# Expert weight slots read in longer contiguous rows: down slots of two experts by 256 features, gate and up slots of neighbouring channels

## The reference, cut to what matters

```python
def expert_choice_moe(xn, w_router, w_gate, w_up, w_down):
    cap = EC_CAPACITY_FACTOR * T // N_EXPERTS                 # 32
    aff = jax.nn.softmax((xn @ w_router), axis=-1)
    g, idx = lax.top_k(jnp.swapaxes(aff, 1, 2), cap)
    xs = xn[bidx, idx]                                        # (1, 16, 32, 1024)
    hid = jax.nn.silu(jnp.einsum('becd,edf->becf', xs, w_gate)) * jnp.einsum('becd,edf->becf', xs, w_up)
    y = jnp.einsum('becf,efd->becd', hid, w_down) * g[..., None]
    return jnp.zeros_like(xn).at[bidx, idx].add(y)
```

## Time and profile before

| | |
|---|---|
| median of 3 runs | 2414.48 us (2411.99 to 2416.81) |
| the profiled execution | 2415.41 us, span of its instructions 2413.6 us |
| mean granted TensorE clock | 0.948 |
| bytes read from HBM | 660.86 MB, of which the experts 402.7 MB |
| the mixture, first matmul L1391 to last L1414 | 409.6 to 1518 us |

### The profile page before, as it was taken

One profiled execution on the slowest core, in us unless ns is written; L12 is line 12 of the kernel. 1 busy time (PEld: TensorE's weight loads), 2 busy tenths in 40 slices (PEclk: granted clock), 3 DMA queues, 4 the chain that ended last, 5 costly groups with the idle time before them and its releaser, 6 DMA issues. The chain is left out here.

```text
span 2413.6 us, 32989 instructions
## 1 busy us (share of the span) xinstructions
PE 2087.0 (86%) x14348; PEld 1443.7 (60%) x14348; DVE 541.1 (22%) x1174; ACT 403.5 (17%) x737; POOL 185.0 (8%) x182
## 2 busy tenths in 40 slices
PE   6998888887687888888788787897999999899997
PEld 2674455554244545665356443674888877478886
DVE  4433432010332200000000210256300023632001
ACT  1122002021121200000000220235300023331001
POOL 0025000000100000000000000026000002330000
PEclk9999898999889999998999999999999999899999
DMA  9459757999999999999999999630254742124450
GB/s 371 162 212 377 283 197 309 412 400 413 409 401 410 415 403 408 412 409 412 405 414 416 415 390 409 202 132 1 95 185 120 164 161 97 60 71 140 130 158 26
DMA packets 239559, 664.03 MB, mean 275 GB/s; under 512 B 18359, under 2 KB 129368, under 8 KB 197112
## 3 DMA queue, kind: packets, MB, share of 16 engines
q1 hardware_dynamic: 239416, 661.93, 71.9%
HBM read 660.86 MB, written 1.05 MB: 274 GB/s over the span
## 5 line engine op out<-in xcount | busy, mean ns | idle before, releaser
L1045 PE MATMUL ps<-arena,ring 128*128 128x256 f32 x2240 | 484.8, 380 | 3.2 <-DVEq L370 3.2
L1045 PEld LDWEIGHTS ps<-arena,ring 128*128 128x128 f32 x2240 | 425.8, 190 | 62.0 <-DVEq L370 4.8
L608 PE MATMUL ps<-arena,ring 128*128 128x256 f32 (+2 forms) x1552 | 353.2, 389 | 15.1 <-DMA ring<-in_w_ffn_in 8.3
L1391 PE MATMUL ps<-ring,arena 128*32 128x256 f32 x4032 | 264.4, 410 | 85.9 <-DMA ring<-in_w_up 53.0
L608 PEld LDWEIGHTS ps<-arena,ring 128*128 128x128 f32 (+2 forms) x1552 | 278.1, 185 | 98.2 <-DMA ring<-in_w_ffn_in 22.1
L1391 PEld LDWEIGHTS ps<-ring,arena 128*32 128x32 f32 x4032 | 126.9, 116 | 209.6 <-DMA ring<-in_w_up 69.0
L1414 PE MATMUL ps<-ring,arena 128*32 128x512 f32 x1024 | 143.2, 684 | 88.1 <-DMA ring<-in_w_down 82.4
L1962 ACT ACTIVATE arena<-ps 128x512 f32<-128x512 f32 (+3 forms) x137 | 74.7, 545 | 774.7 <-PE ps L608 409.9
L1414 PEld LDWEIGHTS ps<-ring,arena 128*32 128x32 f32 x1024 | 29.6, 117 | 177.7 <-DMA ring<-in_w_down 118.5
L1118 PE MATMUL ps<-arena,ring 128*128 128x256 f32 x512 | 113.6, 384 | 5.0 <-issue 5.0
L1118 PEld LDWEIGHTS ps<-arena,ring 128*128 128x128 f32 x512 | 98.3, 193 | 22.2 <-issue 9.0
(11 more groups left out here) (338 smaller groups left out, 1771.3 us busy)
## 6 DMA issues: line engine op xcount, KB each, us to landing
ring<-in_w_up SPq DMA_DIRECT2D x64, 2048.0 KB, 14.0
ring<-in_w_down SPq DMA_DIRECT2D x64, 2048.0 KB, 15.1
ring<-in_w_gate SPq DMA_DIRECT2D x62, 2048.0 KB, 13.3
ring<-in_w_ada SPq DMA_DIRECT2D x36, 2048.0 KB, 12.1
ring<-in_w_ffn_in SPq DMA_DIRECT2D x64, 1024.0 KB, 7.9
ring<-in_w_ffn_out SPq DMA_DIRECT2D x16, 1408.0 KB, 7.0
ring<-in_w_in SPq DMA_DIRECT2D x9, 2048.0 KB, 9.1
ring<-in_w_out SPq DMA_DIRECT2D x6, 2048.0 KB, 7.8
```

The lines of the kernel that those rows point to most:

```text
L608: m = mm(o, a, x, start=(k == 0 and r == 0), stop=(k == kt - 1 and last))
L1045: m = mm(b, w[:, k, c:c + P], src[:, k, :], start=(k == 0), stop=(k == kt - 1))
L1391: m = mm(b[u][32 * c:32 * c + 32, T * x:T * x + T], xs[:, 2 * h + k, CAP * e:CAP * e + CAP], w[:, k, at_:at_ + T], start=(h == 0 and k == ...
```

## The change

Three sizes of row change, and with them the order of channels and features inside the slots. The number of slots, their bytes, their order in the stream and their places stay.

- Gate and up: slot h still holds channels 256h to 256h+255, but partition p now has channels 256h+2p and 256h+2p+1, which are neighbours in HBM: 16 KB in one piece for a partition, and the whole slot is 2 MiB in one piece.
- To match, the stationary operand of the `xs` matmuls takes every second channel of a block of 256 (stride of two floats).
- Down: a slot holds two experts and 256 features; partition p has features 256i+2p and 256i+2p+1 of each, 8 KB in one piece for each expert. Slots alternate between expert pairs a = 0 and 1.
- The transposes of `turn_hidden` take every second column of `hidm`.
- The down matmuls are as many and as large as before; bank a now holds the two experts of pair a, the column half n on partitions 64n to 64n+63. DVE empties each bank with two copies of 64 partitions x 512 columns in place of one of 128 x 512, so that `ysb` looks as before.
- Bank 0 of a group is closed by the last but one slot, bank 1 by the last.

```diff
--- before.py
+++ after.py
@@ -497,12 +497,13 @@
         for s, (kind, i) in enumerate(STEPS):
             if kind == "down":
                 g = i // 8
-                w = I["w_down"][0, 4 * g:4 * g + 4].rearrange("e (f p) n -> p f e n", p=P)
-                stream += [(f"down{g}_{f}", w[:, f]) for f in (2 * (i % 8), 2 * (i % 8) + 1)]
+                for a in range(2):
+                    w = I["w_down"][0, 4 * g + 2 * a:4 * g + 2 * a + 2].rearrange("e (f p s) n -> p f e (s n)", p=P, s=2)
+                    stream.append((f"down{g}_{2 * (i % 8) + a}", w[:, i % 8]))
             else:
                 e = i // 2
-                w = I["w_" + kind][0, e].rearrange("(k p) n -> p k n", p=P)
-                stream += [(f"{kind}{e}_{h}", w[:, 2 * h:2 * h + 2, :]) for h in (2 * (i % 2), 2 * (i % 2) + 1)]
+                w = I["w_" + kind][0, e].rearrange("(h p s) n -> p h s n", p=P, s=2)
+                stream += [(f"{kind}{e}_{h}", w[:, h]) for h in (2 * (i % 2), 2 * (i % 2) + 1)]
             if s in CTX_AT:
                 stream += CTX_STAGES[CTX_AT[s]][1]
         n_moe = len(stream)
@@ -1364,7 +1365,8 @@
             for k in range(KD):
                 b = open_bank(pe, f"xs{k}", MIX_BANKS)
                 for t in range(TT):
-                    m = mm(b[:], htok[:, t, P * k:P * k + P], sel[:, t].rearrange("p e s -> p (e s)"), start=(t == 0), stop=(t == 1))
+                    by_parity = htok[:, t].rearrange("p (h f s) -> p h s f", h=4, s=2)
+                    m = mm(b[:], by_parity[:, k // 2, k % 2], sel[:, t].rearrange("p e s -> p (e s)"), start=(t == 0), stop=(t == 1))
                 close_bank(m, f"xs{k}")
             for g2 in range(2):
                 if g2 == 0:
@@ -1402,22 +1404,25 @@
                 b = open_bank(pe, f"hd{e}", TURN_BANKS)
                 for u in range(2):
                     for x in range(2):
-                        m = nc.tensor.transpose(b[:, P * (2 * u + x):P * (2 * u + x) + P], hidm[u][:, P * x:P * x + P], ident)
+                        m = nc.tensor.transpose(b[:, P * (2 * u + x):P * (2 * u + x) + P], hidm[u].rearrange("p (f s) -> p s f", s=2)[:, x], ident)
                 close_bank(m, f"hd{e}")
 
             def down(g, f, b):
+                i, a = f // 2, f % 2
                 w = take(f"down{g}_{f}")
                 pe.wait_ge(hdt_ready, 4 * g + 4)
-                ch = 8 * (f // 8) + 4 * (f % 2) + f % 8 // 2
-                for n in range(2):
-                    for j in range(4):
-                        m = mm(b[n][32 * j:32 * j + 32, :], hdT[:, j, ch, :], w[:, j, W * n:W * n + W], start=(f == 0), stop=(f == 15))
-                    if f == 15:
-                        close_bank(m, f"dn{g}{n}")
-                if f < 15:
+                for odd in range(2):
+                    ch = 8 * (i // 4) + 4 * odd + i % 4
+                    for n in range(2):
+                        for j in range(2):
+                            at_ = D * odd + W * n
+                            m = mm(b[a][64 * n + 32 * j:64 * n + 32 * j + 32, :], hdT[:, 2 * a + j, ch, :], w[:, j, at_:at_ + W],
+                                   start=(i == 0 and odd == 0), stop=(i == 7 and odd == 1))
+                if i < 7:
                     release(m)
                 else:
-                    release_with(f"dn{g}1")
+                    close_bank(m, f"dn{g}{a}")
+                    release_with(f"dn{g}{a}")
 
             def combine(g, r, banks):
                 pe.wait_ge(ct_ready, 2)
@@ -1936,7 +1941,8 @@
                 elif kind == "down" and i % 8 == 7:
                     for n in range(2):
                         b = read_bank(dve, f"dn{g}{n}")
-                        step(v.tensor_copy(ysb[:, W * n:W * n + W], b[:]), frees=f"dn{g}{n}")
+                        step(v.tensor_copy(ysb[64 * n:64 * n + 64, 0:W], b[0:64, :]))
+                        step(v.tensor_copy(ysb[64 * n:64 * n + 64, W:2 * W], b[64:128, :]), frees=f"dn{g}{n}")
                         tell(y_evac)
                 ctx_stage(s)
             step(ts(A2[X], mod2[:, 0, 8:16, X], 1.0, None, ALU.add))
```

## The result

The changed kernel took 2398.18 us (median of 4, 2396.77 to 2400.21) beside 2415.24 us for the kernel before: ratio 0.9947, 95% interval 0.9925 to 0.9969 (the two medians alone would give 0.9929). That is 13 us less (7 to 18); 15.0 had been forecast. In a second set, with more runs of each, it was 0.9935 (0.9915 to 0.9955). The median of the first four runs lies 17 us lower, but the kernel before spreads over 2402 to 2419 us in what follows, so the ratios are the better measure.

The account below looks back on a forecast made before the run. The mixture was taken to be bound by how fast the 16 DMA engines move bytes. Of 18.6 us saved 15.8 arrive, less 0.8 for the evacuation: -15.0 us, 2399.5 us, range 2391 to 2411.

Parts of the forecast that it names:

- The bound: In the mixture of experts, time goes by how fast the 16 DMA engines move bytes; 409 GB/s from 420 to 1500 us.
- rival (2): PE takes the gain: faster loads wait more often for one of four ring places; 2413 to 2416 us; chance 0.10.
- The price of a row: Each row of a load costs a DMA engine 9.1 ns, beside 151.5 ns for 4 KB of bytes.
- Adjacent dimensions are merged: A partition's two neighbouring rows are sent as one piece though the view names them separately; 239559 packets less 32768.
- The down term: Down slots: 32768 rows of 4 KB become 16384 of 8 KB, saving each engine 9.3 us; bounds 8.6 to 12.4.
- the factor 0.87: Share of the loads' saving that arrives in the mixture: 13% is lost, so 18.2 us become 15.8.
- seven windows: Windows of 20 us with DMA share 0.97 to 0.99 in six, 0.89 in one; savings inside these 140 us are lost.
- The gate and up term: Gate and up slots: half as many rows, 16 KB for 8 KB, saving each engine 9.3 us; bounds 0 to 11.9.
- The evacuation: End of the last group: bank 1 takes two DVE copies of 0.69 us each, +0.8 us; bounds 0 to 0.8.
- The strided loads: Strided stationary operands of L1367 and the transposes: 0 us taken; upper bounds 6 us and under 1 us.
- (1): Half of the gain: 16 KB pieces bring nothing, or half of the 9.1 ns isn't the row's; 2407.2 us; chance 0.19.
- (3): Gate and up loads: 16 KB from partition to partition is bad spacing for memory; +11.5 us, 2426.0 us; chance 0.09.

Follow-up runs that it names:

- the part alone: Only the down change, or only the gate and up change, made to the kernel before: ratio 0.9964 (8.7 us less) and 0.9971 (7.0 us less).
- the ACT experiment: Changed kernel with ACT copying one half of the very last bank while DVE copies the other: ratio 0.9948 to the kernel before.
- the run of one expert: Changed kernel, but a down slot is one expert by 512 features in four 4 KB rows: ratio 0.9998 to the kernel before.

## Why the prediction was right

**The bound.** Right. In the down phases, and in the third and fourth of gate and up, time followed the bytes' rate in both directions (4, 8 and 16 KB). The waits of the earlier trace rows are those of PE and of its weight load together, as the first part of the prediction says; rival (2) is argued there with all 402 us, of which half is nearer to lost time.

**The price of a row.** Right. From 408, 421 and 427 GB/s an engine takes 160.6, 311.3 and 613.9 ns for a row of 4, 8 and 16 KB, so a row costs 9.9 ns by the first two and 8.8 by the last two, where 9.1 was taken. Neither the number of experts in a slot nor a contiguous slot had a part in it. Whether the price is that of the piece itself or of the jump to another address, no run separates.

**Adjacent dimensions are merged.** Right, 32768 packets fewer.

**The down term.** 8.1 us were to arrive (9.3 x 0.87). The down phases of the two traces of after are 8.3 us shorter than the mean of the three of before, and the part alone gained 8.7 (5.5 to 12) in time. That the factor 0.87 fits is luck: of the seven windows behind it none lies in a down phase.

**The gate and up term.** 7.7 us were to arrive (8.9 x 0.87). In time the part alone gained 7.0 (3.6 to 10.4), which agrees. In the traces it is 731.4 to 726.4, 5.0 us, and 7.2 in the trace of the part alone. The sum was about right; the way to it was not. The prediction lost only what falls inside seven windows of 20 us, 13% of the stretch, and kept "what they saved before". Six of the seven (from 420, 480, 500, 680, 700 and 740 us) lie in the first and second phase, 120 of their 353 us, so two thirds of the 4.6 us saved there were to be kept; by the traces above it is 0.9 us. The third and fourth passed on all of their 2.3 us each (2.7 and 2.4), though the seventh window lies in the fourth. The whole mixture became 11 to 13 us shorter, where 15.8 was to arrive. The rows: phases 1 to 4 of gate and up, first in the second trace of before, then after.

```profile
403.50:580.50 177.00, 150.55 (x1439) 98.67 (x1440) 16.23 (x29) 31.07 (x50) 0.00 (x0) 0.94 0.99 398
...
669.00:844.30 175.30, 144.87 (x1401) 93.19 (x1401) 45.04 (x103) 39.28 (x86) 0.00 (x0) 0.98 1.01 414
...
942.50:1138.10 195.60, 168.03 (x1473) 117.12 (x1472) 12.06 (x23) 9.65 (x19) 0.00 (x0) 0.95 1.02 412
...
1236.60:1418.50 181.90, 152.92 (x1429) 101.78 (x1429) 24.72 (x51) 28.43 (x49) 0.00 (x0) 0.95 1.02 413
```

```profile
408.00:585.20 177.20, 147.89 (x1436) 97.63 (x1436) 16.22 (x29) 31.07 (x50) 0.00 (x0) 0.96 0.98 401
...
672.00:847.50 175.50, 148.03 (x1401) 94.65 (x1400) 45.05 (x103) 38.22 (x83) 0.00 (x0) 0.97 1.00 409
...
943.70:1136.50 192.80, 167.77 (x1473) 116.40 (x1472) 12.07 (x23) 9.65 (x19) 0.00 (x0) 0.95 1.01 417
...
1231.70:1413.00 181.30, 148.82 (x1429) 99.97 (x1428) 24.72 (x51) 28.36 (x49) 0.00 (x0) 0.98 1.01 417
```

In the third and fourth phase the rate rose from 412 and 413 to 417; in the second it did not rise (407 to 414 in the three traces of before, 409 in after), and the share is 1.00. In one place of it the DMA engines stand idle for part of the time, while PE works:

```profile
684.00:692.00 8.00, 6.96 (x80) 4.03 (x79) 3.10 (x7) 1.32 (x6) 0.00 (x0) 1.00 0.97 379
692.00:700.00 8.00, 7.54 (x96) 4.28 (x98) 2.56 (x6) 4.69 (x11) 0.00 (x0) 1.00 0.93 352
```

The timeline names what holds the places there (the changed kernel, PE, one step of two slots):

```profile
684.23 3.66 PE L1393 MATMUL ps<-ring,arena 128*32 128x256 f32 x64
687.82 1.13 PE L1432 MATMUL ps<-arena 128*128 128x256 f32 x4
688.88 1.13 PE L816 MATMUL ps<-arena 64*128 64x256 f32 x4
691.05 0.66 PE L824 MATMUL ps<-tab,arena 128*128 128x128 f32 x4 [1.04 <-DVE arena L2542]
...
695.82 4.52 PE L1393 MATMUL ps<-ring,arena 128*32 128x256 f32 x80
```

Slots of one step begin at 684.23, those of the next at 695.82: 11.6 us for two slots which the engines deliver in 10 (2 x 2 MiB at 420 GB/s); the same step takes 12.0 us in the kernel before (677.40 to 689.42). Between them stand the combine of the group before and the scores, transposes and values of the context attention, with two waits each for DVE's softmax. That is rival (2), true in this place. It was not taken out of the kernel to see the gain come through, and PE still waits for slots elsewhere in both phases, so that this is what kept the gain of the second phase is argued and not shown, and more so for the first, where the rows show 0.98 to 0.99 and no single place is named.

**The evacuation.** Right: +0.72 us, where 0.8 was taken, and by the ACT experiment 0.60 of it is the second copy.

**The strided loads.** Taken at nothing, and they cost nothing that shows, though not because the loads are equally fast. The changed kernel's:

```profile
L1407 PEld LDWEIGHTS ps<-tab,arena x64: 194/204/230, 444.4 to 1411.8; 128*128 128x128 f32 x64
```

```profile
L1369 PEld LDWEIGHTS ps<-arena x32: 195/197/337, 390.3 to 404.8; 128*128 128x128 f32 x32
```

141 became 204 ns in the transposes, 14 ns above the bound of 190, 4 us for 64 records where 3 was the worst; 190 became 197 in L1369, and its 32 records still take 15.5 us in all.

**Rivals.** (1), half of the gain, fell by the rates, that of the run of one expert among them. The rule of the Trainium skill in "DMA: Bandwidth & Descriptors", section "Why small descriptors are slow (HBM only)", an overhead of some 3 cycles for each packet, which the prediction made 3.5 ns for a row, does not cover it: by that estimate, made from the section's 3 cycles and the page's 850 MHz, the gate and up slots of 4 KB would have cost 7 us, and they cost 17 (12 to 22). The section names a second overhead, 32 B for each DMA operation, which the prediction left out; at 32 B a beat that is an estimate of 1.2 ns more, too little as well. (3), a bad spacing, did not show: 427 GB/s at 16 KB from partition to partition.

## What to carry to other kernels

Where the DMA engines are full, count the rows of a load and not only its bytes: take the rate of two pure stretches with different rows, work out the price of one row, and fetch neighbouring channels into one partition if the other operand can be permuted for free. How much of it arrived differed from phase to phase; where little does, compare the length of PE's step between two slots with the time of their load, which the share of busy time over a window hides. Take the rate from stretches long enough for many rows: 8 us gave 426 for rows of 8 KB and 428 to 430 for rows of 16 KB. And compare ratios and several traces where less than a percent is at stake: the mixture of the kernel before differed by 7 us from one trace to another, and a trace can be that of the fastest execution, 10 us under the median.

## What the runs showed of the hardware

- A DMA row costs an engine some 9 ns beside its bytes, 9.9 ns by the rates of 4 and 8 KB rows (408 and 421 GB/s) and 8.8 by those of 8 and 16 KB (421 and 427); a piece of 16 KB is one packet.
- A moving operand in float32 with 8 B from element to element takes 388 ns for 256 columns against 379 without stride, with 16 B 632 ns. For a stationary operand 8 B made 197 of 190 ns and 204 of 141 ns: strided, both forms end at about 200.
- A DVE copy from PSUM of 64 partitions x 512 takes 0.68 to 0.69 us, as that of 128 x 512 did; ACT takes 0.59 for it.
